# Writing the sliding-window cache copies from DRAM to DRAM in the mLSTM stage instead of from SBUF page slots in the selected-attention stage

## The reference

```
def layer_c_sample(x, c, page_table, ..., win_k, win_v, ...):
    ...
    kw_all = jnp.concatenate([win_k.astype(kw.dtype), kw], axis=1)   # 512 cached + 8 new positions
    vw_all = jnp.concatenate([win_v.astype(vw.dtype), vw], axis=1)
    o = nsa_attend(q, pos, gates, kc, vc, c_end, overlap, fetch_sel, kw_all, vw_all, kw_pos)
    y = nsa_output(...)
    return y, kcr, vcr, ks, vs, kw_all[:, T:], vw_all[:, T:]         # the window caches are outputs
```

## Time and profile before

| what | value |
|---|---|
| median of three runs | 1518.5 us (1514.65 to 1519.91) |
| the profiled execution | 1517.92 us |
| its span | 1516.3 us |
| TensorE, matmul busy | 1290.0 us, 85% of the span |
| VectorE, ScalarE, GpSimd busy | 465.9, 405.3, 156.7 us |
| mean granted TensorE clock | 0.901 of full speed |
| moved by DMA | 233.79 MB: SP's queue (q1) 156.67, GpSimd's (q0) 75.51, instructions (q8, q14) 1.60 |

### The profile page before, as it was taken

One profiled execution on the slowest core, in us unless ns is written; L12 is line 12 of the kernel. 1 busy time (PEld: TensorE's weight loads), 2 busy tenths in 40 slices (PEclk: granted clock), 3 DMA queues, 4 the chain that ended last, 5 costly groups with the idle time before them and its releaser, 6 DMA issues. The chain is left out here.

```text
span 1516.3 us, 25300 instructions
## 1 busy us (share of the span) xinstructions
PE 1290.0 (85%) x9349; PEld 827.1 (55%) x9349; DVE 465.9 (31%) x1448; ACT 405.3 (27%) x1059; POOL 156.7 (10%) x289
## 2 busy tenths in 40 slices
PE   4699999975959859999998899999997777678694
PEld 2476755733637625567778455555554333345473
DVE  0342120005561130202201755555552332222113
ACT  2211111121210120000111456555653333334100
POOL 0000000010000000000001222222223322221000
PEclk9799999995779979999995899999998878788798
DMA  6514332340022301113003666666658888876201
GB/s 287 222 57 166 111 111 111 112 166 11 1 63 79 132 24 56 56 56 149 1 0 111 232 224 223 223 225 236 235 204 325 329 312 333 303 284 224 112 0 62
DMA packets 73062, 233.79 MB, mean 154 GB/s; under 512 B 9578, under 2 KB 14828, under 8 KB 66924
## 3 DMA queue, kind: packets, MB, share of 16 engines
q1 hardware_dynamic: 50156, 156.67, 28.9%
q0 software_dynamic: 22784, 75.51, 13.3%
HBM read 215.10 MB, written 17.05 MB: 153 GB/s over the span
## 5 line engine op out<-in xcount | busy, mean ns | idle before, releaser
L368 PE MATMUL ps<-arena,wring 128*128 128x288 f32 x1920 | 480.8, 410 | 22.4 <-DMA wring<-in_weights 14.1
L368 PEld LDWEIGHTS ps<-arena,wring 128*128 128x128 f32 x1920 | 366.0, 192 | 131.6 <-DMA wring<-in_weights 14.5
L1421 POOL DMA_DIRECT2D arena<-in_cmp_pages x128 | 70.0, 547 | 512.7 <-issue 300.0
L375 PE MATMUL ps<-wring,arena 128*128 128x512 f32 (+1 forms) x240 | 107.0, 604 | 15.7 <-ACT arena L455 15.7
L1955 ACT ACTIVATE arena<-arena 128x512 f32<-128x512 f32 (+1 forms) x88 | 57.1, 651 | 145.3 <-DVE arena L1991 145.3
L375 PEld LDWEIGHTS ps<-wring,arena 128*128 128x128 f32 (+1 forms) x240 | 43.1, 183 | 75.6 <-issue 59.7
L1515 DVE CUSTOM_DVE_ANT_0 wring<-ps,wring 128x128 f32<-128x128 f32 (+3 forms) x128 | 57.6, 487 | 77.0 <-PE ps L1444 75.2
L1919 PE MATMUL ps<-fixed,arena 128*128 128x128 f32 x288 | 57.5, 338 | 19.0 <-ACT arena L1955 18.9
L1507 ACT ACTIVATE wring<-ps 128x128 f32<-128x128 f32 (+3 forms) x128 | 49.0, 435 | 91.3 <-PE ps L1467 91.3
L1493 ACT ACTIVATE wring<-wring 128x128 f32<-128x128 f32 (+3 forms) x128 | 70.7, 559 | 8.8 <-DVE wring L1515 8.7
L1580 PE MATMUL ps<-arena 128*32 128x256 f32 x1024 | 70.4, 393 | 0.0
(11 more groups left out here) (345 smaller groups left out, 1503.3 us busy)
## 6 DMA issues: line engine op xcount, KB each, us to landing
wring<-in_weights SPq DMA_DIRECT2D x30, 2048.0 KB, 8.2
arena<-in_cmp_pages POOLq DMA_DIRECT2D x128, 256.0 KB, 4.4
arena<-in_cmp_pages SPq DMA_DIRECT2D x128, 256.0 KB, 3.4
arena<-in_kv_pages SPq DMA_DIRECT2D x64, 256.0 KB, 9.1
arena<-in_kv_pages POOLq DMA_DIRECT2D x64, 256.0 KB, 7.3
wring<-in_kv_pages SPq DMA_DIRECT2D x64, 256.0 KB, 9.6
wring<-in_kv_pages POOLq DMA_DIRECT2D x64, 256.0 KB, 7.5
wring<-in_win_kv SPq DMA_DIRECT2D x4, 1024.0 KB, 15.3
```

Source lines behind the costliest of these rows:

```text
L368: last = pe.matmul(out[:, 0:HT], w[:, k, ct * P:ct * P + P], moving[k][:, half * HT:half * HT + HT], start=(k == 0), stop=(k == KT - 1))
L375: last = pe.matmul(main[0:m, :], moving[k][:, index * P:index * P + m], w[:, k, :], start=(k == 0), stop=(k == KT - 1))
L1421: eng.dma_start(cring[q % CR][:, 2 * half + j, :], v["cmp_pages"][bass.ds(ids[2 * d + j], 1)] .rearrange("o p c -> (o p) c")).then_inc(c_i ...
```

## The change

The sixteen stores leave the GpSimd queue and the selected-attention block. SP issues sixteen transfers in their place in the mLSTM block, right after the load of `state_C`, and their source is the input tensor `win_kv` in DRAM and no longer a slot in SBUF. The window is still loaded into its slot for the attention. The wait on `win_out` before a load into the slot goes away; the wait of GpSimd at the end of the long block stays.

```
@@ mLSTM block @@
+        win_out = sem("win_out")
...
             def _(sp):
                 sp.dma_start(caug[:, :, :, 0:HD].rearrange("p b h e -> p (b h) e"), v["state_C"]).then_inc(in_c, 16)
+                for b in range(NB):
+                    sp.dma_start(v["win_k_out"][b], v["win_kv"][b, :, 0:2 * TP]).then_inc(win_out, 16)
+                    sp.dma_start(v["win_v_out"][b], v["win_kv"][b, :, 2 * TP:]).then_inc(win_out, 16)
                 sp.wait_ge(dve_m, DV["staged"])
@@ selected attention @@
-        win_out = sem("win_out")
...
                 eng.wait_ge(pe_s, at4(PS_, n0, ("pv", JS.index(i0))))
-                if i0 == NG:
-                    eng.wait_ge(win_out, 32 * (n0 + 1))
...
-        def store_window(eng, n):
-            eng.wait_ge(kv_in[0][(n * NL + NG) % KS], kv_total[0, n, NG])
-            eng.dma_start(v["win_k_out"][n], kv_slot(n, NG)[:, 0:2 * TP]).then_inc(win_out, 16)
-            eng.dma_start(v["win_v_out"][n], kv_slot(n, NG)[:, 2 * TP:]).then_inc(win_out, 16)
...
                     for pair in range(NG // 2):
                         load_kv(pool, 1, n, pair)
-                        if n and pair == 1:
-                            store_window(pool, n - 1)
-                store_window(pool, NB - 1)
                 pool.wait_ge(win_out, 32 * NB)
```

## The result

| | before | after |
|---|---|---|
| median of the runs | 1516.86 us (4 runs, 1514.65 to 1519.91) | 1497.03 us (4 runs, 1496.22 to 1499.38) |
| the profiled execution, its span | 1517.92, 1516.3 us | 1496.22, 1494.5 us |
| mean granted TensorE clock | 0.901 | 0.910 |

The ratio after to before is 0.9865, with a 95% interval of 0.9843 to 0.9887. The change makes the kernel 19.8 us faster by the medians. 1.6 us of this are not the change's: the kernel before has one run more here, and its median is 1516.86 and no longer the 1518.5 from which the forecast was worked out.

A forecast was written before the change was run, and what follows sets the result against it. The prediction took DMA load bursts at 384 GB/s, delaying each window in the selected attention, as the bound. 13.4 - 0.3 - 0.7 = 12.4 us less than 1517.92 gave 1505.5, so a median of 1506 us, range 1499 to 1516.

The forecast's parts named there:

- Item 1: Selected attention: stores leave the load bursts, saving 2.2 us per period, capped by TensorE's waits; 13.4 us in all.
- all waits gone: Selected attention: all 20.2 us of TensorE's waits for pages and window vanish; 1499 us, the range's lower end.
- Item 5: Head of the mLSTM block: copies queued behind the state's load delay it by 0.3 us, at most 5.5.
- Item 7: mLSTM stage: the copies' load delays instruction fetches, a third of one 2.2 us gap, 0.7 us.
- Item 2: Selected attention: dropped waits before the store and on `win_out` gain nothing; TensorE's 2.29 us exponential wait per sample stays.
- the first rival: Selected attention: more than the store's own time is gained, through TensorE's clock; 17 to 20 us, about 1500; chance 0.08.
- the hole: Start of each burst: idle DMA time without the store could cost up to 1.2 us of the saving.
- Items 2 to 4: Dropped window and `win_out` waits, POOL's final wait, and sixteen SP issues (10 us) each change the time by nothing.
- Item 6: mLSTM stage: the copies take about 45 us, half the loads' rate, all hidden while the DMA engines are idle.
- Handed back: Selected attention: slower clock stretches and idle burst starts use up the gain; 2.5 us less, 1516; chance 0.17.
- outlast their stage: mLSTM stage: slow copies delay the `C_s` store; at 60 GB/s 28 us slower, 1546; chance 0.09, shared with state and fetch costs.
- DMA share in slices 10 and 11: Profile sign for the mLSTM stage, where the DMA engines were nearly idle: a share of several tenths.

The follow-up runs named there:

- no copies: The changed kernel without the sixteen transfers and the wait for them, window outputs left unwritten; 1496.4 us, ratio 0.9872.
- store in the pause: The kernel before with the slot store issued one pair of groups earlier on GpSimd's queue; 1494.1 us, ratio 0.9865.
- copies before the state: The changed kernel with the sixteen copies queued in front of the state's load on SP's queue; 1528.9 us, ratio 1.0066.
- half of it moved: The changed kernel with only the keys copied in the mLSTM stage and the values still stored from the slot; 1510.2 us, ratio 0.9954.
- extra copies: The kernel before, its stores kept, plus sixteen copies to a scratch tensor behind the state's load; 1518.7 us, ratio 1.0006.
- the store doubled: The kernel before with each window stored twice from its slot, the second time to a scratch tensor; 1528.9 us, ratio 1.0078.
- the clock alone: The kernel before with four matmuls on constants before TensorE's wait for the first exponentials of samples 1 to 7; 1514.8 us, ratio 0.9975.
- loads held: The changed kernel with GpSimd waiting for the previous sample's window before its half of the next sample's first groups; 1485.5 us, ratio 0.9781.

## Why the prediction was right and wrong

**Item 1, the failed step.** It priced the store's bytes rightly: 2.2 us per period taken, 2.2 measured as the shortening of a burst. What failed is the sentence behind it, "A period cannot gain more than TensorE waits in it". By it the last sample was given 0.3 us, the whole item came to 13.4 where the bursts gave 15.6, and "all waits gone" became the lower end of the range. The last burst shortened by 2.5 us and the last period by as much, at a wait of 0.3 to 0.4 us before and after. The other kernels show that this is no accident of one profile. The last period is 27.5 to 28.5 us in the four kernels without the store in the last burst (after, no copies, store in the pause, copies before the state), 28.8 with half of it moved, 31.0 and 30.4 with the store as before (before, extra copies), and 33.1 with the store doubled. With the clock raised it is 29.1 without the store and 31.0 with it. As long as the window is late, its landing sets the period in this loop, and TensorE's account fills up to it: with waits for loads, with a lower clock, with gaps on "issue". A shorter burst takes from any of them; the run with the clock alone shows the reverse, a higher clock and 9 us more of waits. Without the cap the item is 7 x 2.2 = 15.4 and the forecast 1503.5, so the cap is the mechanism that was wrong but only 2 us of the miss.

**What remains, and the second failed step.** The forecast was 12.4 us less, and the two profiled executions differ by 21.7. The bursts gave 2.2 more than item 1; the pauses 2.9 and the two ends 1.4, for which the sum had no term; the 1.0 us of cost of items 5 and 7 did not come; 1.8 lie outside the stretch, in parts that scatter by as much. The largest of these is the pauses. Item 2 let the chain behind the window stay as it was, and its wait for the exponentials did stay. But the four products of the window with which that chain starts took 1.72 to 1.98 us in five of the seven samples and after the change 1.08 in six of them, 11.72 and 8.45 us in all. These 3.3 us are about the size of the 2.9. It is the clock at one place in the chain, which the first rival had asked for ("some 3 to 5 us of slow clock"). I do not call it shown: no run raised the clock at just these products, and the sum of the pauses differs by up to 10 us between kernels in which no instruction of the chain was changed (34.1 to 44.3). In the kernel with the store doubled these products took 11.1 us and the pauses only 34.1.

**Item 1, the hole.** The hesitant start was meant to cost up to 1.2 us. 1.05 MB at the 0.37 MB/us of a whole burst is 2.8 us; 2.2 came back, so 0.6 were lost there, where the item's 2.2 of 2.7 had taken 0.5. That fits.

**Items 2 to 4.** As said: no wait on `win_out` or for the last store mattered, and SP's sixteen issues, 16 us with the long first one, were hidden behind 85 us of slack.

**Item 5, the state's load.** 0.3 taken, 0.06 measured. The copies placed in front of it show that the order of issue protects it.

**Item 6, the copies' rate.** 45 us taken for 8.4 MB, about 25 measured. The guess that each byte read and written in the same memory halves the rate was wrong here: state and copies together moved at 315 GB/s. The Trainium skill, page "DMA: Bandwidth & Descriptors", section "Latency and other measured facts", has 207 to 214 GB/s for copies between HBM tensors, in rows of 16 KiB at a pitch of 512 KiB and at one of 4 MiB plus 4 KiB. The rows here are 4 KB at 8 KB, so it is another form; for this one the measurement decides, and it is over that. Nothing hung on it, with 100 us to hide in.

**Item 7, fetches.** 0.7 taken; the extra copies cost nothing that can be measured, and the block has no gap on "issue" of that size. By the rule cited there (the Trainium skill, page "Runtime: NRT & Kernel Launch", section "Instruction fetch mechanics") the item was to be 0, and in this block the runs agree. In the loaded samples the gaps stayed (11.2 us in the changed kernel, 15.1 with the loads held, 7 to 9 in four others). That they are fetches behind data is not shown.

**The rivals.** "More than the store's own time" came nearest in its number, 1500, and had 0.08. Its mechanism, the clock, is refuted for the bursts, which make 15.6 of the 19.95 us: with a higher clock they are as long as before. For the 2.9 us of the pauses it stands open, as said. "Handed back" did not happen, though half moved shows that pauses can take half of a gain. The copies did not outlast their stage: they were over 67 us early.

**The signs named beforehand.** Waits for loads between 5 and 9 us: wrong, 12.4. Products of the window every 31 to 32 us: 28.5 to 32.9. Bursts about 2 us shorter and the state's wait: right. The mLSTM stage within 1 us of its length: 1.2 us longer, within its scatter. DMA share in slices 10 and 11: only the tenth, since the copies were twice as fast as taken.

## What to carry to other kernels

Where loads come in bursts at the engines' limit and the last load of a burst starts the chain that frees the next slots, count the bytes that are moved ahead of that load, from all queues; here each 1.05 MB there made a burst 2.2 us longer, whether or not the busiest engine seemed to wait that long. The busiest engine's waits are then no upper bound of a gain, since its clock and its other gaps stretch into the same time: 20.2 us of waits were there, and the change and the held loads together took 35.6 out of the stretch. The burst is not the whole period, though; the pause behind it took back part of the effect in two runs and added to it in the change. Before bytes are moved to another stage, try to let them wait: one line earlier in the queue gave as much here as the whole move, one wait nearly as much, and the move and the wait together more.

## What was not expected of the hardware

- DRAM to DRAM copies behind a load of 2 MB, with the DMA engines otherwise idle: 315 GB/s over 32 us, the load included. The same transfers at the head of a burst of loads, from GpSimd's queue: a share down to 0.54 at 173 GB/s, and 7.9 us more in the medians than with the source in SBUF.
- The issue on SP's queue right behind the load of the state took 6.12 us, each further one 0.6; with the copies in front of the state the first took 0.67. The issue behind the store of `C_s` took 5.41 us before the change.
- A clock of 0.87 for 0.81 over 266 us of the main engine's work moved the time by 0.25% (0.05% to 0.46%).
